# Two tile pairs per gate-up phase moved from whole products to seven-product groups, with the token sums made earlier

## The reference

```
h = rms_norm(x, gain)
f = (silu(h @ w_gate) * (h @ w_up)) @ w_down      # w_gate, w_up: 1024 x 2816, w_down: 2816 x 1024
```

## Time and profile before

| what | us |
|---|---|
| median of 3 runs | 1138.45 (1137.72 to 1138.57) |
| the profiled execution's own time | 1139.19 |
| its span, first to last instruction | 1137.1 |
| PE busy / DVE busy / ACT busy | 1108.9 / 784.6 / 599.8 |
| mean granted TensorE clock | 0.997 |

### The profile page before, as it was taken

The page is one execution under the profiler, slowest core; times in us unless marked ns, Lnnn a source line. Parts: engine busy times, 40 slices in busy tenths (PEclk is TensorE's granted clock), DMA queues, the critical chain, the costliest instruction groups (busy, mean ns, idle before and its releaser), DMA issues.

```text
span 1137.1 us, 17312 instructions
## 1 busy us (share of the span) xinstructions
PE 1108.9 (98%) x6568; PEld 965.0 (85%) x6568; DVE 784.6 (69%) x1304; ACT 599.8 (53%) x1067; POOL 120.4 (11%) x143
## 2 busy tenths in 40 slices
PE   8999989999999999999999999999999999999997
PEld 6688767997899999888898887787889999988886
DVE  6788886767998888533378688563688888872333
ACT  6787884546455556422254468542545555562231
POOL 1476743000000000000000004200000000000000
PEclk9999999999999999999999999999999999999999
DMA  7323313213233333433323211022321333343212
GB/s 283 107 69 92 91 42 111 95 56 100 86 105 100 112 112 112 130 97 107 110 67 111 93 58 36 20 94 61 124 93 59 117 104 112 112 132 109 93 56 74
DMA packets 34145, 109.24 MB, mean 96 GB/s; under 512 B 4368, under 2 KB 7056, under 8 KB 33936
## 3 DMA queue, kind: packets, MB, share of 16 engines
q1 hardware_dynamic: 33312, 107.22, 29.0%
q10 hardware_dynamic: 752, 0.92, 0.3%
HBM read 100.78 MB, written 2.10 MB: 90 GB/s over the span
## 4 chain that ended last, share of the span: by engine, by line
PE 87%; DVE 5%; ACT 4%; issue 2%; POOL 1%; DMA 1%; ACTq 0%; SPq 0%; DVEq 0%; POOLq 0%
PE bank L539 16%; PE bank L541 15%; PE bank L540 15%; PE bank L2078 8%; PE bank L2077 8%; PE bank L2079 8%; PE bank L1046 2%; PE bank L1056 2%; PE bank L1129 1%; PE bank L1001 1%; PE bank L1003 1%; PE bank L1002 1%; PE bank L1131 1%; PE bank L1130 1%; DVE wl L460 1%
## 5 line engine op out<-in xcount | busy, mean ns | idle before, releaser
L460 DVE TENSOR_TENSOR wl<-raw,wh 128x1024 fp32r<-128x1024 f32 x125 | 154.1, 1238 | 188.5 <-ACT wh L452 188.4
L452 ACT ACTIVATE wh<-raw 128x1024 fp32r<-128x1024 f32 x125 | 130.9, 1053 | 205.8 <-PE bank L541 190.3
L2079 PE MATMUL bank<-h,wl 128*128 128x256 f32 x784 | 222.1, 283 | 0.0
L2078 PE MATMUL bank<-h,wh 128*128 128x256 f32 x784 | 221.7, 283 | 0.0
L2077 PE MATMUL bank<-h,wh 128*128 128x256 f32 x784 | 221.0, 282 | 0.5 <-ACT acc L2384 0.5
L539 PE MATMUL bank<-hh,wh 128*128 128x512 f32 x424 | 170.4, 402 | 3.5 <-DVE wl L460 3.1
L541 PE MATMUL bank<-hh,wl 128*128 128x512 f32 x424 | 165.9, 391 | 0.0
L540 PE MATMUL bank<-hl,wh 128*128 128x512 f32 x424 | 165.8, 391 | 0.0
L2077 PEld LDWEIGHTS bank<-h,wh 128*128 128x128 f32 x784 | 148.3, 189 | 1.2 <-ACT acc L2384 0.9
L2079 PEld LDWEIGHTS bank<-h,wl 128*128 128x128 f32 x784 | 147.9, 189 | 0.0
L2078 PEld LDWEIGHTS bank<-h,wh 128*128 128x128 f32 x784 | 147.5, 188 | 0.1
(11 more groups left out here) (285 smaller groups left out, 2226.5 us busy)
## 6 DMA issues: line engine op xcount, KB each, us to landing
raw<-weights SPq DMA_DIRECT2D x181, 512.0 KB, 3.6
xres<-x_t SPq DMA_DIRECT2D x8, 512.0 KB, 6.2
sw<-ta SPq DMA_DIRECT2D x36, 64.0 KB, 2.0
out_t<-final SPq DMA_DIRECT2D x6, 256.0 KB, 2.3
q<-sw SPq DMA_DIRECT2D x10, 128.0 KB, 2.3
q<-ta SPq DMA_DIRECT2D x10, 128.0 KB, 2.3
rope<-angles SPq DMA_DIRECT2D x1, 1024.0 KB, 10.3
sw<-ta ACTq DMA_DIRECT2D x4, 64.0 KB, 3.1
```

Source lines behind the costliest of these rows:

```text
L452: act.activation(wh[:, j, :, :], raw[:, j, :, :], ACT.Copy).then_inc(high_split, 1)
L460: v.tensor_tensor(wl[:, j, :, :], raw[:, j, :, :], wh[:, j, :, :].bitcast(F32), ALU.subtract)\
L2078: pe.matmul(o, wh_half[:, h, k, :], h7[:, p, 1, k, :], start=False, stop=False, skip_group_check=True)
L2079: ins = pe.matmul(o, wl_half[:, h, k, :], h7[:, p, 0, k, :], start=False, stop=k == HK - 1, skip_group_check=True)
```

## The change

PLAIN goes from 8 to 6: pairs 6 and 7 of each phase are made as seven-product groups, so there are 16 groups. The hand-written orders of ACT and DVE are redone for the shorter row of whole pairs. The buffer `gwhole` grows from 14 to 16 tiles (the size of `hh` and `hl` together, over which it lies); `EARLY_SPLIT` stays 8, so the hidden tiles 6 and 7, which now come from groups 0 and 1, are split in groups 2 and 3.

```diff
-PLAIN = 8
+PLAIN = 6
 GROUPS = FT - PLAIN
-TOKENS_ACT = ("11", "12", "22", "21", P1, P2, P5, P6, P7, P4, P3)
+TOKENS_ACT = ("11", "12", "22", "21", P1, P2, P6, P5, P7, P4, P3)
-        gwhole = place("gwhole", [P, FT - EARLY_SPLIT, S], at=hh_at)
+        gwhole = place("gwhole", [P, FT - PLAIN, S], at=hh_at)
...
             for f in range(PLAIN - 1):
                 vec_gate(v, gu, f)
                 vec_product(v, gu, f)
-                for c in {0: (6,), 1: (7, 8), 2: (9, 10), 3: (11, 12), 4: (13, 14), 5: (15,)}.get(f, ()):
+                for c in {0: (6,), 1: (7, 8), 2: (9, 10), 3: (11,)}.get(f, ()):
                     vec_split(v, gu.c0 + c)
                 vec_hidden_low(v, gu, f)
-                for t in {2: ("11", "12", "d1"), 3: ("22", "t2", "21"), 4: ("d3", "t4")}.get(f, ()):
+                for t in {1: ("11",), 2: ("12", "d1", "22"), 3: ("t2", "21", "d3", "t4")}.get(f, ()):
                     vec_token(v, gu, t)
-                for p in {4: (P1,), 5: (P2, P6, P5), 6: (P7,)}.get(f, ()):
-                    vec_seven(v, gu, p)
-                if f == 5:
-                    vec_sum13(v, gu, 0)
-                if f == 6:
-                    vec_unit(v, gu, 0, "12")
-                    vec_s2(v, gu, 0)
-                    vec_s4(v, gu, 0)
-                    vec_seven(v, gu, P4)
-                    vec_seven(v, gu, P3)
-            for m in range(GROUPS - 1):
+            for p in (P1, P2, P6):
+                vec_seven(v, gu, p)
+            vec_sum13(v, gu, 0)
+            vec_unit(v, gu, 0, "12")
+            vec_s2(v, gu, 0)
+            vec_s4(v, gu, 0)
+            vec_seven(v, gu, P5)
+            vec_first_group(v, gu)
+            for m in range(1, GROUPS - 1):
                 vec_group(v, gu, m)
...
+        def vec_first_group(v, gu):
+            vec_gate(v, gu, PLAIN - 1)
+            vec_unit(v, gu, 0, "24")
+            vec_product(v, gu, PLAIN - 1)
+            vec_unit(v, gu, 0, "13")
+            vec_c11(v, gu, 0)
+            vec_seven(v, gu, P7)
+            vec_hidden_low(v, gu, PLAIN - 1)
+            vec_unit(v, gu, 1, "12")
+            vec_unit(v, gu, 0, "22")
+            vec_sum13(v, gu, 1)
+            vec_c22(v, gu, 0)
+            vec_seven(v, gu, P4)
+            vec_s2(v, gu, 1)
+            vec_s4(v, gu, 1)
+            vec_seven(v, gu, P3)
...
+            if m >= 2 and PLAIN + m - 2 < EARLY_SPLIT:
+                vec_hidden_low(v, gu, PLAIN + m - 2)
...
         def act_gate_up(act, gu, gain):
             for f in range(PLAIN - 1):
                 act_silu(act, gu, f)
-                if f < 4:
-                    act_tokens(act, gu, gain, TOKENS_ACT[f])
-                for c in {0: (6,), 1: (7, 8), 2: (9, 10), 3: (11, 12), 4: (13, 14), 5: (15,)}.get(f, ()):
+                for t in {0: ("11", "12"), 1: ("22",), 2: ("21",)}.get(f, ()):
+                    act_tokens(act, gu, gain, t)
+                for c in {0: (6,), 1: (7, 8), 2: (9, 10), 3: (11,)}.get(f, ()):
                     act_split(act, gu.c0 + c)
-                if f == 6:
+                act_hidden_high(act, gu, f)
+                for p in {2: (P1,), 3: (P2, P6), 4: (P5, P7)}.get(f, ()):
+                    act_seven(act, gu, p)
+                if f == 3:
                     act_unit(act, gu, 0, "12")
-                act_hidden_high(act, gu, f)
-                for p in {3: (P1,), 4: (P2, P5), 5: (P6, P7), 6: (P4, P3)}.get(f, ()):
-                    act_seven(act, gu, p)
+            act_seven(act, gu, P4)
             act_unit(act, gu, 0, "24")
-            for m in range(GROUPS - 1):
+            act_unit(act, gu, 0, "13")
+            act_silu(act, gu, PLAIN - 1)
+            act_c1(act, gu, 0)
+            act_hidden_high(act, gu, PLAIN - 1)
+            act_unit(act, gu, 1, "12")
+            act_unit(act, gu, 0, "22")
+            act_group_silu(act, gu, 0, 0)
+            act_u1(act, gu, 0)
+            act_seven(act, gu, P3)
+            act_c5(act, gu, 0)
+            act_unit(act, gu, 1, "24")
+            for m in range(1, GROUPS - 1):
                 act_group(act, gu, m)
```

More of the change, by code:

```diff
@@ L2292, in vec_group @@
         def vec_group(v, gu, m):
-            if m == 0:
-                vec_gate(v, gu, PLAIN - 1)
-            vec_c22(v, gu, m - 1)
+            if m > 1:
+                vec_c22(v, gu, m - 1)
             vec_unit(v, gu, m, "24")
-            if m == 0:
-                vec_product(v, gu, PLAIN - 1)
             vec_unit(v, gu, m, "13")
             vec_c11(v, gu, m)
-            if m == 0:
-                vec_hidden_low(v, gu, PLAIN - 1)
             vec_sum13(v, gu, m + 1)
@@ L2350, in act_hidden_high @@
                 reached(act, gu.product, PLAIN + 2 * (f - PLAIN) + 2)
-                freed = (P1, P2, P6, P5, P7, P3, P4)[(f - PLAIN) // 2]
-                reached(act, gu.multiplied, MULTIPLIED[GROUPS - 1, freed])
+                if f >= EARLY_SPLIT:
+                    freed = (P1, P2, P6, P5, P7, P3, P4)[(f - EARLY_SPLIT) // 2]
+                    reached(act, gu.multiplied, MULTIPLIED[GROUPS - 1, freed])
             act.activation(gh[:, f, :], hidden_source(f), ACT.Copy).then_inc(gu.hidden_high.of, 1)
@@ L2412, in act_group @@
             act_unit(act, gu, m, "13")
-            if m == 0:
-                act_silu(act, gu, PLAIN - 1)
             act_c1(act, gu, m)
-            if m == 0:
-                act_hidden_high(act, gu, PLAIN - 1)
             act_unit(act, gu, m + 1, "12")
@@ L2421, in act_group @@
             act_u1(act, gu, m)
+            if m >= 2 and PLAIN + m - 2 < EARLY_SPLIT:
+                act_hidden_high(act, gu, PLAIN + m - 2)
             act_group_silu(act, gu, m - 1, 1)
```

## The result

The changed kernel takes 1147.06 us (median of 6 runs, 1145.65 to 1151.74), the kernel before 1138.09 (6 runs, 1136.28 to 1138.57). The ratio is 1.0087, 95% interval 1.0069 to 1.0104: 9.9 us slower (7.9 to 11.8). The medians lie 9.0 us apart, the means (1147.64 and 1137.72) 9.9; one run of 1151.74 has a part in that. Forecast were 1148.2 us, 9.8 more than before, in a range of 1144.5 to 1151.

A forecast was written before the change was run, and what follows sets the result against it. The prediction took PE to bound the kernel, busy 98% of the span. Waits less PE's saving gave +8.5 us in phase 1 and +1.3 in phase 2: 1138.45 + 9.8 = 1148.2 us, range 1144.5 to 1151.

The forecast's parts named there:

- PE's saving: Pairs made as seven-product groups: 0.80 us of PE work saved a pair, 1.6 a phase, 3.2 in all.
- Tile 6: Phase 1, pair 0: two ACT token blocks delay chunk 6's split, so PE waits until 260.9, 1.6 us more.
- Wait 1: Phase 1, before P1 of group 0: PE ready at 293.9, DVE's unit 12 at 297.3, 3.5 us.
- Waits 2 and 3: PE waiting for DVE's unit 24: 1.9 us before P6 of group 0 (phase 1), 2.2 before P6 of group 1 (both phases).
- The small waits between them: Phase 1, between P6 of group 0 and P6 of group 1: PE following DVE, 0.3, 0.2, 0.1 and 0.3 us.
- Nothing later: From group 2 on: DVE caught up, no waits, low parts of tiles 6 and 7 fit the slack.
- The sum: Whole kernel: +8.5 us in phase 1 and +1.3 in phase 2, together +9.8.
- the fall of the clock: Rival: PE's clock falls in the new waits before tile 6 and P1; 1148.5 to 1150.6 us, chance 0.12.
- DVE staying behind beyond group 1: Rival: P6 of groups 2 and 3 waits too, up to 1.0 us a phase; 1149 to 1150.5 us, chance 0.08.
- only the head waits staying: Rival: the wait before P6 of group 1 and the small ones vanish, +3.8 us; 1142.3 us, chance 0.08.
- The faster side: Rival: token blocks 11 and 12 made in ACT's idle time, only chunk 6's wait left; 1136.9 us, chance 0.05.

The follow-up runs named there:

- e5: Kernel before (eight whole pairs), ACT making token blocks 11 and 12 both ahead of chunk 6's split, 22 and 21 in the next pairs: 1141.59 us, ratio 1.0031.
- e1: Changed kernel (six pairs) with ACT's chunk splits and high copy ahead of the token blocks in pairs 0 to 3: 1144.22 us, ratio 1.0044 to the kernel before.
- e4: Kernel before (eight whole pairs) with ACT's splits ahead of the token block of each pair: 1136.89 us, ratio 0.9980.
- e8: The kernel before, unchanged, profiled a second time: 1139.87 us, one run.
- e6: Changed kernel (six pairs) with ACT's and DVE's lists of pairs 0 to 4 rewritten: 1138.11 us, ratio 0.9997 to the kernel before.
- e7: Changed kernel with low parts of P7, P4, P3 and ACT's copy for P3 moved ahead of pair 5's gates: 1150.98 us, ratio 1.0113 to the kernel before.
- e2: Changed kernel with the low parts of P5, P7, P4 and P3 moved from DVE to POOL: 1160.69 us, ratio 1.0191 to the kernel before.

## Why the prediction was right

- **PE's saving, 3.2 us.** Its sign holds and its size was a little low. In phase 2, where PE is not kept waiting for P1, it starts P1 67.68 us after the factor before and 45.91 after the change: 21.77 us less for four tiles. From P6 of group 1 to the down phase it takes 148.7 us in place of 128.8: 19.9 for two groups. That saves 1.8 us a phase, 3.7 in all. The price of 10.08 us a group was read in the phase with the longer interval (120 ns); at 119.2 a group is 10.01. (The matmuls are 84 for 48, 1.75 times as many and not twice, as the prediction words it; its sum uses the right numbers.)
- **Tile 6.** Start 260.82 (forecast 260.9), wait 3.30 (3.3). e5 shows the price of this alone with eight pairs, e1 and e4 that the edit of one order takes it away.
- **Wait 1.** P1 at 297.43 (297.4), unit 12 ready at 297.32 (297.3). The wait on PE was 2.03 (3.5), because the clock had fallen after tile 6.
- **Waits 2 and 3.** P6 of group 0 at 302.22 (302.2), P6 of group 1 at 314.22 (314.0); waits 1.71 (1.9) and 2.14 (2.2). The small waits between them come to 1.1 us (0.9), by the difference to the same stretch before (from P6 of group 0 to P6 of group 1 12.00 - 2.14 us, before 8.81). In phase 2 no wait 1 and 2, and 2.14 for wait 3 (2.2).
- **Nothing later.** From P6 of group 1 on, PE takes 148.7 us for 1248 matmuls, 119.2 ns each, with no wait but one of 0.28 in the last group that the kernel before has too (0.22): DVE had caught up, and the low parts of tiles 6 and 7 were hidden.
- **The sum.** From the factor to the down phase, phase 1 of the changed kernel takes 462.94 - 253.46 = 209.5 us and phase 2 1012.57 - 802.99 = 209.6. Against the first profile of the kernel before that is 7.1 and 1.5 us more, against e8 8.5 and 0.2: 8.6 and 8.7 together, where 9.8 was forecast. In each of these two profiles one phase has the interval of 120.5 ns. Phase by phase, against the one without it, it is +8.5 and +1.5 (forecast +8.5 and +1.3). So the walk of the queues is right, and that the whole came out at 9.9 is in part luck: PE's saving was 0.5 us larger than forecast, P6 of group 1 came about 0.3 us later than forecast in each phase, and the mean of the changed kernel holds one run of 1151.74. The second way in which the prediction adds phase 1 up (1.6 + 3.5 + 1.9 + 0.9 + 2.2 - 0.3 - 1.6) gives 8.2 and not 8.5; the forecast rests on the first.

The rows on which the first and the last point rest, from the timeline of PE in the changed kernel (first matmul of the down phase, P1 of phase 2, the second down phase):

```profile
462.94 0.39 PE L539 MATMUL bank<-gsplit,wh 128*128 128x512 f32 x1
...
848.90 0.28 PE L2077 MATMUL bank<-h,wh 128*128 128x256 f32 x1
...
1012.57 0.40 PE L539 MATMUL bank<-gsplit,wh 128*128 128x512 f32 x1
```

The same two starts of the down phase in the first profile of the kernel before:

```profile
455.91 0.40 PE L539 MATMUL bank<-gsplit,wh 128*128 128x512 f32 x1
...
1004.14 0.39 PE L539 MATMUL bank<-gsplit,wh 128*128 128x512 f32 x1
```

Of the rivals, the fall of the clock took place, but only where the prediction said it would be absorbed; from 297 to 320 the clock was 1.00, so it was right for the profiled execution to give it no price. For some executions that may be too low: the run of the changed kernel with a mean clock of 0.991 took 1151.74 us, the five with 0.995 to 0.997 took 1145.65 to 1148.01. That run has no trace. DVE staying behind beyond group 1 and only the head waits staying are both excluded by the trace. The faster side, made by e6 in the way that the prediction described, ends at no change and not at 1136.9: of the 10.1 us in which DVE idled much can be won, but wait 2 takes its place, since DVE's work up to P6 of group 1 is longer than PE's. e7 fits that from the other side.

## What to carry to other kernels

When the bound engine's work is shortened, look up what the other engines must finish before its next kind of work begins, and add their lists up: here 3.7 us of PE work were saved, and some 13 us of waits and of lower clock came, because the work of DVE between the norm and group 1 shrank less than PE's. In a list worked in order, an instruction that feeds the bound engine goes ahead of one that is needed later; this one edit was worth 4.9 us with six pairs and 2.3 with eight. An idle engine is only free if its work does not hold up the busy one, as POOL's held up DVE's here.

## What the runs showed of the hardware

- Instructions of 128x1024 with two operands in SBUF hardly overlapped on DVE and POOL: beside POOL's of 3.2 us, DVE's of 1.22 us became 3.35 (e2).
- A wait of 3.30 us on PE was followed by the lower clock in the profiles of the changed kernel, e2 and e7 and not in that of e5, and one of 3.24 us in phase 2 of e7 was not; after the waits of 2.92 us in e6 and 5.11 us in e7 the clock was 0.50 for about 6 us. The runs of the changed kernel also spread more, which fits this: 1145.65 to 1151.74 for the changed kernel, 1136.28 to 1138.57 for the kernel before beside it.
- The start-to-start time of 256-column matmuls was 119.2 or 120.5 ns over a whole phase at a granted clock of 1.00, and in the two profiles of the kernel before the longer one stood in different phases.
